# First FFN: 32 modulation sums from GpSimd to VectorE, step by step between its other work

## What is computed

```python
c_act = jax.nn.silu(c)
for layer in range(DEPTH):                       # DEPTH = 2
    mod = c_act @ mod_w[layer] + mod_b[layer]    # 1024 -> 6 * 1024
    sh1, sc1, g1, sh2, sc2, g2 = jnp.split(mod, N_MOD, axis=-1)
    ...                                          # mixer, h = h + g1 * mix
    u = modulate(rms_norm(h, norm_ffn[layer]), sh2, sc2)
    h = h + g2[:, None, :] * swiglu(u, ffn_w_in[layer], ffn_w_out[layer])
    if layer == N_A_LAYERS - 1:                  # after layer 0
        k_pad, v_pad = shared_kv(h, c_act, kv_norm, kv_mod_w, kv_mod_b, kv_w)

def swiglu(u, w_in, w_out):
    gate, up = jnp.split(u @ w_in, 2, axis=-1)   # 1024 -> 2 * 2816
    return (jax.nn.silu(gate) * up) @ w_out      # 2816 -> 1024
```

## Time and profile before

| | us |
|---|---|
| median of 3 runs | 2476.05 |
| lowest and highest | 2466.85, 2478.48 |
| profiled execution | 2478.46 |
| its span, first to last instruction | 2476.5 |
| mean granted TensorE clock | 0.951 of 2.4 GHz |
| TensorE products busy | 2268.3 |
| VectorE busy | 1403.7 |
| ScalarE busy | 763.8 |
| GpSimd busy | 418.8 |

### The profile page before, as it was taken

How to read it: one execution, slowest core, us unless ns; L and a number is a source line. 1 busy time by engine, 2 the same in 40 slices (tenths; PEclk the granted TensorE clock), 3 DMA queues, 4 the chain that set the end, 5 groups by cost and what they waited for, 6 DMA issues and landing times.

```text
span 2476.5 us, 25507 instructions
## 1 busy us (share of the span) xinstructions
PE 2268.3 (92%) x10056; PEld 1808.9 (73%) x10056; DVE 1403.7 (57%) x1854; ACT 763.8 (31%) x977; POOL 418.8 (17%) x272
## 2 busy tenths in 40 slices
PE   8899999889999979999899999788898876999996
PEld 5688888677888868766788888566476664888885
DVE  6577665547767672455544444563544555555556
ACT  1443333322222232345322222353123232322221
POOL 0000000089889732000000000000400000000000
PEclk9899999899999989999999999889889887999998
DMA  6243231245554523210222222122022311222220
GB/s 259 103 152 106 99 119 52 69 153 187 187 187 170 187 86 144 90 35 24 81 98 92 102 102 87 69 68 85 0 68 78 109 68 52 102 86 101 101 87 34
DMA packets 39645, 252.66 MB, mean 102 GB/s; under 512 B 4563, under 2 KB 4755, under 8 KB 11048
## 3 DMA queue, kind: packets, MB, share of 16 engines
q1 hardware_dynamic: 33176, 234.11, 26.8%
q0 software_dynamic: 3008, 10.63, 1.4%
q10 hardware_dynamic: 3344, 6.29, 0.7%
HBM read 244.73 MB, written 6.29 MB: 101 GB/s over the span
## 4 chain that ended last, share of the span: by engine, by line
PE 82%; DVE 9%; issue 4%; POOL 2%; ACT 2%; DMA 1%; SPq 0%; ACTq 0%; DVEq 0%; POOLq 0%
PE bank L635 23%; PE bank L637 22%; PE bank L636 22%; PE bank L848 2%; PE bank L950 2%; PE bank L960 1%; PE bank L938 1%; DVE w_lo L1552 1%; PE bank L682 1%; DVE scr L1582 1%; PE bank L764 1%; PE bank L1029 1%; PE bank L758 1%; POOL raw L550 1%; DVE scr L1620 1%
## 5 line engine op out<-in xcount | busy, mean ns | idle before, releaser
L635 PE MATMUL bank<-u_hi,w_hi 128*128 128x512 f32 x1772 | 714.7, 403 | 46.8 <-DVE u_lo L1614 11.2
L636 PE MATMUL bank<-u_lo,w_hi 128*128 128x512 f32 x1772 | 701.5, 396 | 0.0
L637 PE MATMUL bank<-u_hi,w_lo 128*128 128x512 f32 x1772 | 701.1, 396 | 0.0
L1552 DVE TENSOR_TENSOR w_lo<-raw,w_hi 128x2048 fp32r<-128x2048 f32 x165 | 435.1, 2637 | 306.0 <-ACT w_hi L1123 305.9
L635 PEld LDWEIGHTS bank<-u_hi,w_hi 128*128 128x128 f32 x1772 | 340.5, 192 | 129.5 <-issue 47.8
L1123 ACT ACTIVATE w_hi<-raw 128x2048 fp32r<-128x2048 f32 x165 | 314.9, 1909 | 342.9 <-PE bank L637 306.9
L637 PEld LDWEIGHTS bank<-u_hi,w_lo 128*128 128x128 f32 x1772 | 339.5, 192 | 73.0
L636 PEld LDWEIGHTS bank<-u_lo,w_hi 128*128 128x128 f32 x1772 | 340.6, 192 | 67.8 <-issue 0.2
L635 PE MATMUL bank<-g_hi,w_hi 128*128 128x512 f32 x708 | 281.7, 398 | 20.3 <-DVE w_lo L1552 12.6
L636 PE MATMUL bank<-g_lo,w_hi 128*128 128x512 f32 x708 | 278.9, 394 | 0.0
L637 PE MATMUL bank<-g_hi,w_lo 128*128 128x512 f32 x708 | 278.6, 393 | 0.0
(11 more groups left out here) (249 smaller groups left out, 2317.7 us busy)
## 6 DMA issues: line engine op xcount, KB each, us to landing
raw<-in_wts SPq DMA_DIRECT2D x221, 1024.0 KB, 4.9
spectra<-pool ACTq DMA_DIRECT2D x16, 256.0 KB, 2.0
pool<-in_rel POOLq DMA_DIRECT2D x16, 256.0 KB, 2.9
pool<-spectra POOLq DMA_DIRECT2D x16, 256.0 KB, 3.0
H<-in_x ACTq DMA_DIRECT2D x1, 2048.0 KB, 20.7
out<-H SPq DMA_DIRECT2D x1, 2048.0 KB, 7.1
pool<-in_window POOLq DMA_DIRECT2D x1, 1024.0 KB, 8.9
pool<-in_filt_w POOLq DMA_DIRECT2D x1, 512.0 KB, 5.8
```

The costliest lines, as they stand in the source:

```text
L635: pe.matmul(out, lh, rh, start=start, stop=False, skip_group_check=True)
L636: pe.matmul(out, lh, rl, start=False, stop=False, skip_group_check=True)
L637: return pe.matmul(out, ll, rh, start=False, stop=stop, skip_group_check=True)
L1552: dve.tensor_tensor(w_lo[w % hi_ring][:, :], raw[W_STREAM[w] % raw_ring][:, :], w_hi[w % hi_ring][:, :].bitcast(F32), ALU.subtract).then_i ...
```

## The change

The constant `M_POOLED` grows by 32, so that pieces 20 to 51 are no longer GpSimd's. VectorE sums them by `sum_mod`, eight steps each, in its FFN program: in an `fi` slot all eight steps of a piece after the product into `ff_h`, in an `fo` slot one step behind each residual addition. Which piece belongs to a slot is `placed`: the one that stands right behind the slot's weight in the stream. The stream changes in one place: there is no piece behind `fi` 0, and there are two behind `fi` 2. GpSimd sums only 52 to 55, and begins when the input of the K/V projection is written (`U_KV + KC`) and no longer at the FFN's input.

```diff
-M_POOLED = M_DIRECT + M_HOOKED
+M_POOLED = M_DIRECT + M_HOOKED + 32
...
-            m = min(left[0], 2 if label == "fi" and i == 1 else 1) if layer == "0" else 0
+            m = min(left[0], {("fi", 0): 0, ("fi", 1): 2, ("fi", 2): 2}.get((label, i), 1)) if layer == "0" else 0
...
-MOD_POINTS = [(M_DIRECT, 2), (M_POOLED, 5), (24, 6), (52, 13), (NM, NVMOD)]
+MOD_POINTS = [(M_DIRECT, 2), (M_DIRECT + M_HOOKED, 5), (24, 6), (52, 13), (NM, NVMOD)]
...
             def sum_mods():
-                pl.wait_ge(u_l, U_FFN0 + KC)
+                pl.wait_ge(u_l, U_KV + KC)
                 for m in range(M_POOLED, NM):
...
             def ffn(layer, gcount, sg, gate, mixer, after):
+                def placed(label, i):
+                    w = W_AT[(label + layer, i)]
+                    return [(m, k) for m in range(M_DIRECT + M_HOOKED, M_POOLED) if M_BEFORE[m] == w + 1 for k in range(KC)]
...
                             dve.tensor_tensor(ff_h[:, i % 2, :], ff_s[:, i % 2, :], read(n + 1)[:, :], ALU.mult).then_inc(free["dve"], 1)
+                            for m, k in placed("fi", i):
+                                sum_mod(m, k)
...
                             if c == 1:
                                 ahead(f"fo{layer}", g - 1)
+                            for m, k in placed("fo", g - 1)[c::KC]:
+                                sum_mod(m, k)
```

## The result

The changed kernel takes **2575.05 us** (median of 4 runs, 2573.25 to 2579.3), the kernel before on the same chip 2471.61 (4 runs, 2466.85 to 2478.48). The ratio is 1.0417, 95% interval 1.0391 to 1.0443: slower by 103 us by the medians; the forecast was 2570 us, 2545 to 2605. The profiled execution took 2575.53 us (span 2573.7, mean clock 0.940), against 2478.46 (2476.5, 0.951) before: +97.1.

What follows compares the result with a forecast made beforehand. TensorE, busy 92% of the span, was taken to bound the kernel before. FFN +95, norm -5.1 and last four sums +3.5 made +93.4 us: 2572 from the profiled 2478.46, forecast 2570 us given the median 2476.05, range 2545 to 2605.

Steps and rivals of the forecast that it cites:

- The loop: First FFN: 9.1 us from freed buffer to usable weight adds to VectorE's own work, 14.3 us per `fi` slot.
- group: Two `fi` slots and one `fo` slot of the first FFN: predicted 44.9 us, against 34.76 before.
- coupling: After an `fo` slot, the next `fi` product is ready some 0.4 us after VectorE could take it, through TensorE's seventh bank.
- The `fo` loop: First FFN's `fo` slot: seven steps and six residuals, 6.8 us, then 9.1, together 15.9 us.
- Rival 3: Waits lower TensorE's clock for half the next slot: 3.7 us in each of nine groups, 33 in all, 2603; chance 0.08.
- Start: First FFN's first weights: `fi` 2 ready at 512.9, `fi` 3 at 538.0, `fo` 0 at 556.3, `fi` 4 at 570.6.
- End of the FFN: TensorE's last product of the first FFN at 984 instead of 889.0, a difference of +95 us.
- Norm: Between last FFN product and the norm's column sums, 8.68 us before: 5.1 us less, as GpSimd's sums wait.
- Last four sums: K/V stage: GpSimd's later start makes TensorE stall at `kk` 2, 0 to 7 us, taken as +3.5.
- The signs: Changed profile: TensorE 88 or 89% busy, FFN waits 90 us or more, groups 44 to 45, VectorE idle 5 to 7 before `w_lo`.
- Busy time: VectorE in the first FFN: 121 us of steps added against 96 given back, up a few per cent, so it fits.
- Rival 1: Faster: first-FFN weights arrive in time and freeing VectorE of GpSimd pays, gain 17.9 us, 2458; chance 0.04.

Runs made afterwards that it cites:

- experiment 7: The changed kernel, but in the first FFN's `fo` slots VectorE makes the next `w_lo` after the sixth residual instead of the second: 2529.48 us.
- 1: The changed kernel, but VectorE sums each of the 32 pieces one slot earlier: 2466.73 us, ratio 0.9973 to the kernel before.
- 5: The kernel before, GpSimd still summing, but each first-FFN sum waits until VectorE passes the place of the changed kernel's steps: 2749.83 us.
- experiment 10: The kernel of 9, with the last four sums also on VectorE, in the `kk` slots: 2446.96 us, ratio 0.9891 to the kernel before.
- Experiment 3: The changed kernel with GpSimd's start for the last four sums put back to the FFN's input: 2576.8 us.
- 9: The kernel of 8, with each `fo` slot's eight steps placed behind residuals six, seven and eight (two, three, three): 2452.46 us.
- 8: The kernel of 1, with the next `w_lo` in the first FFN's `fo` slots after the fourth residual instead of the second: 2469.76 us.
- experiment 2: The kernel of 1, with VectorE also summing the last four pieces in the `kk` slots: 2466.97 us, ratio 0.9978 to the kernel before.

## Why the prediction held, point by point

- **The loop.** As predicted: a load starts with the sum's last step, and its weight is usable 9.1 us later (experiment 7: 653.75 to 662.87 is 9.1). Of the two `fi` loops of a group, the one that ends with the next `fi` weight takes 14.2 us (14.3 predicted), the one that ends with the `fo` weight 14.9 in the mean (14.3 and 0.4 of coupling predicted). Experiments 1 and 5 show it to be the cause, from both sides: open it and the loss goes, build it into the kernel before and it comes.
- **The `fo` loop was mis-sized: 15.9 predicted, 16.6 measured** (mean of nine, 15.9 to 18.0; the expectation of experiment 7 puts 17.0). The term that was too small is "seven steps and six residuals, 6.8 us": it counted VectorE's instructions and took TensorE's banks as ready. I had seen the wait and the low clock and had put both in TensorE's slack. But banks 6 and 7 are made while TensorE runs at 1.2 GHz, and the last residual waits for them if that lasts long. In the loop shown above the clock is low until about 666.8 (0.77 over the window from 665 to 669 is 1.84 us at half speed and the rest at full), that is for 5.9 us after the restart and not 3.5, and the residual waits 0.97 us; a load of 5.89 instead of 4.85 makes the rest of this loop's 18.0. Read in the same way, the nine stretches are 2.9, 3.0, 3.8, 4.0, 4.3, 5.1, 5.9, 5.9 and 6.2 us long, and the residual's waits, in the same order, 0, 0, 0.25, 0.38, 0.51, 0.85, 0.97, 0.97 and 0.97: 0.54 in the mean. The two loops without a wait take 15.9 us, exactly the prediction. (The 7.5 us ahead of `H` in VectorE's rows above hold four more waits, 2.6 us, in the last two `fo` slots, which have no sums.) A group came to 45.75 instead of 44.9; over eight groups 366.0 us instead of 359.2.
- **Rival 3** was wrong on the price. Its condition, the clock low for half a slot, is 5.4 us, and the stretches are 4.6 in the mean, 6.2 at most. But it set down the 5.4 as time lost, and 5.4 us at half speed lose 2.7; to lose 5.4 the clock would have to be low for 10.9. And what is lost in TensorE's slack costs nothing: 0.5 us a group lay on the path, and not 3.7. From 510 to 860 us the clock is 0.90 in the mean and 1.00 in experiment 10. The Trainium skill (TensorE: Matmul & The Clock Gate, "HAM oscillation — how this bites in real kernels") describes the pattern, a wait in each pass and a slow restart behind it; the trace agrees (0.50 behind each of nine waits of 5.0 to 6.6 us, one in each `fo` slot that has sums). Here what such a restart costs depends on who waits for the banks.
- **Start.** `fi` 2, `fi` 3, `fo` 0 and `fi` 4 were ready at 511.3, 536.0, 554.2 and 568.5, against 512.9, 538.0, 556.3 and 570.6. This execution came to the FFN 1.7 us earlier, so the start is right within 0.4.
- **End of the FFN**: last product at 990.6 (994.16 - 3.58), predicted 984: +6.8 from the groups, +1.9 behind `fi` 20, -2.1 from the start.
- **Norm**: -5.1, measured 8.68 to 3.58. **Last four sums**: +3.5; TensorE waits 2.38 us for `kk` 2, and from norm to norm the stage takes 322.1 us instead of 318.6, +3.5. Experiment 3 puts both back and gets nearly the same time.
- **The total is nearer than the stage.** From the norm ahead of the FFN to the norm behind the K/V stage the profiled executions differ by 101.6 us (833.1 against 731.5), where 93.4 was predicted. The whole differs by 97.1, because this execution came to the FFN 1.7 us earlier and took 3.0 less in the second layer (480.1 against 483.1), in code that is the same. That part of the agreement is luck.
- **The signs.** TensorE's share (89%), the idle time ahead of `w_lo` (5.1 to 7.9 us inside the groups), the 2.29 us for `w_lo`, 0.68 for `g_lo` and SyncE's waits are as named. TensorE's waits came to 83.7 us, not 90 or more, and the groups to 45.75, not 44 to 45.
- **Busy time is no bound**: 121 us of steps against 96 given back would be +25. VectorE's busy time, in which overlapping instructions count once, grew by 11.4 us in the FFN (267.7 to 279.2) and by 9.2 over the whole.
- **Rival 1's 18 us** were real, and reachable only with the loop open: 1 got about 6 of them, 9 some 21, with 2.29 us for `w_lo` and 0.68 for `g_lo`. The Trainium skill (SBUF — State Buffer, "Who interferes with whom") gives the cause of the longer times before, an exclusive port pair; the trace agrees, 3.93 and 2.58 us beside GpSimd and 2.29 and 0.68 without.

Not settled: why single loads in the changed kernel take 5.3 and 5.9 us where most take 4.8; and why the clock stays low for 2.9 us in one `fo` slot and 6.2 in another. And of the time that 9 gained over 8, some 4 us lie outside the FFN, in code that is the same.

## What to carry to other kernels

Work that frees a buffer belongs in the program ahead of the wait it serves by at least the time of load and conversion; ask of each in-order list what it frees, who loads into it, and where in the same list the result is waited for. If that is the next instruction, the times add, however idle the engine is. When a wait only moves, count all instructions between the two points that the bound engine cares about, and move out of that stretch what isn't due.

## What the runs showed of the hardware

- A step that reads and writes 8 columns instead of 256 still takes 0.22 us (0.48 before); in a chain of dependent steps each costs about 0.26 less than its 0.52, and between residuals the next instruction starts 0.14 us after it instead of 0.40.
- After a wait of 5.17 us TensorE ran for 5.9 us at 1.2 GHz; after the one of 6.83 us in the kernel before, 3.5 us. The longer wait did not have the longer slow stretch, nor does it within the changed kernel: 3.0 us behind a wait of 5.04, 5.9 behind 5.12, 3.8 behind 6.61. An engine that reads the banks can be held up in one pass and not in the next.
- Equal code differs by several microseconds between executions: the second layer's stretch named in experiment 2 took 473.5 to 483.1 us in the profiled executions, with a mean clock of 0.91 (1) and 0.88 (before) from 1595 to 2040 us. An effect of 3 us is to be looked for in its own stage.
